# Sorted experts: who issues the loads of a block's rows and the stores of its results

## The chip, the cores and the metric

The kernel runs on one core of one Trainium2 chip. The metric is the device time in microseconds (us) of one execution. The kernel before was timed three times: 2738.66, 2728.6 and 2728.08 us, with a median of 2728.6 us.

The engines are named as the profile names them. PE is the matrix engine (PEld its weight load), DVE the vector engine, ACT the scalar engine, POOL is GpSimd, and SP is the synchronising engine, which in this kernel only issues transfers. An engine runs its own list of instructions strictly in order, and a wait on a semaphore holds back everything that stands behind it in that list.

## What is computed

The program is two dense transformer layers (`first_block`, in a loop over `DEPTH`) and then one block whose last part is a mixture of experts. 512 tokens of width 1024 are each sent to 2 of 16 experts:

```
gates = sum(one_hot(e_glob, 16) * weights)            # 2 of 16 per token
a = einsum('td,edf->tef', ht, w_e_gate)               # 1024 -> 256
u = einsum('td,edf->tef', ht, w_e_up)                 # 1024 -> 256
hid = silu(a) * u * gates[:, :, None]
out = hid.reshape(t, 16 * 256) @ w_e_down.reshape(16 * 256, d)
```

Everything is in float32. A product is made of three matrix products: each operand is split into a high part and a rest (`hi`, `lo`), and hi\*hi, lo\*hi and hi\*lo are added up.

## The kernel before

The change lies in `experts`, the last but one stage. The router has given each of the 1024 pairs of token and expert a row number (`slot`). GpSimd scatters the token rows into a table in HBM, `moe_in`, with eight indirect transfers (L2204). The table is sorted by expert and cut into 23 blocks of 128 rows: one block for each of the 16 experts, and 7 spill blocks for experts with more than 128 rows (`BLOCKS = EXPERTS + SPILLS`). For each block b the kernel loads 128 rows of 4 KB (0.52 MB) into `xb[b % 2]`, multiplies them with the weights of the expert, and stores 128 result rows (0.52 MB) from `y[b % 2]` into `moe_out` (L2214). After the last block `combine` gathers the results by eight indirect transfers (L2446). The weights of an expert are three transfers of 1.05 MB: two halves of gate and up (`load_gu`, L1979) and the down matrix (`load_down`, L1983). Weights, rows, results, split operands and sums all have two buffers.

The work of one block, by line:

- PE transposes the rows, `x_turn(b)`, eight operations (L2376); it waits for the load of the rows (`x_in`).
- ACT and DVE split the transposed rows (L2245, L2310) and the weights (L2253 and L2318 for the two halves of gate and up, L2268 and L2331 for down).
- PE makes gate and up, `up(b, 0)` and `up(b, 1)`, 12 matmuls each (L2389). ACT applies silu (L2275), DVE multiplies (`gated`, L2339).
- PE transposes the hidden rows, `h_turn(b)` (L2400), which ACT and DVE split (L2261, L2325).
- PE makes the output, `down(b)`, 12 matmuls (L2412), and ACT and DVE copy one half each into `y` (`y_half`, L2283 and L2347).

The engines are staggered by hand. In its iteration b each runs, in this order:

```
PE   x_turn(b+1)  up(b,0)  h_turn(b-1)  up(b,1)  down(b-1)
ACT  y_half(b-2)  x_hi(b+1)  w_hi(b+1,0)  h_hi(b-1)  w_hi(b+1,1)  down_hi(b)  gate(b)
DVE  y_half(b-2)  x_lo(b+1)  w_lo(b+1,0)  h_lo(b-1)  w_lo(b+1,1)  down_lo(b)  gated(b)
```

SP issues all the plain transfers of the stage. In its iteration b it waits until the rows of block b-2 are transposed and loads the rows of block b, waits for the split of the weights of b-2 and loads the weights of block b, and stores the results of block b-4 (`store_y`). So one list holds three kinds of transfer, and a store stands four blocks behind the load ahead of it. GpSimd does nothing between its eight scatters and the eight gathers of `combine`.

Of the kernel before, what the change touches and what calls it, by code (L numbers as in the profile page):

```python
# [26 lines left out]
P = 128  # L27
SEQ = 512
TB = SEQ // P
# [38 lines left out]
CHOSEN = 2  # L68
SPILLS = (CHOSEN * SEQ - EXPERTS) // P
BLOCKS = EXPERTS + SPILLS  # L70
# [2080 lines left out]
def experts(core, w_moe, rows, slot, spill_of):  # L2151
# [8 lines left out]
    with ExitStack() as st:  # L2160
# [10 lines left out]
        y = [rows[:, s, :] for s in range(2)]  # L2171
        xb = [rows[:, 2 + s, :] for s in range(2)]
# [4 lines left out]
        scattered = core.sem("moe_scattered", st)  # L2177
        x_in = [core.sem(f"moe_x_in{s}", st) for s in range(2)]
        x_turned = core.sem("moe_x_turned", st)
# [3 lines left out]
        gu_lo_done = core.sem("moe_gu_lo_done", st)  # L2183
        d_hi_done = core.sem("moe_d_hi_done", st)
        d_lo_done = core.sem("moe_d_lo_done", st)
# [7 lines left out]
        y_act = core.sem("moe_y_act", st)  # L2193
        y_dve = core.sem("moe_y_dve", st)
        y_out = [core.sem(f"moe_y_out{s}", st) for s in range(2)]
# [3 lines left out]
        with nc.Block() as block:  # L2199
            @block.gpsimd  # L2200
            def _(pool):
                for t in range(TB):
                    for n in range(CHOSEN):
                        nc.gpsimd.indirect_dma_start(  # L2204
                            out=core.moe_in[:, :], out_offset=bass.IndirectOffsetOnAxis(ap=slot[:, n, t:t + 1], axis=0),
                            in_=rows[:, t, :], in_offset=None).then_inc(scattered, 16)

            @block.sync
            def _(sp):
                def store_y(b):  # L2210
                    s = b % 2
                    sp.wait_ge(y_act, b + 1)
                    sp.wait_ge(y_dve, b + 1)
                    sp.dma_start(core.moe_out[b * P:(b + 1) * P, :], y[s]).then_inc(y_out[s], 16)  # L2214

                spills = [sp.value_load(spill_of[0:1, j:j + 1], min_val=0, max_val=EXPERTS - 1) for j in range(SPILLS)]
                sp.wait_ge(scattered, 16 * CHOSEN * TB)
                for b in range(BLOCKS):
                    s = b % 2
                    e = b if b < EXPERTS else spills[b - EXPERTS]  # L2220
                    if b >= 2:
                        sp.wait_ge(x_turned, b - 1)
                    sp.dma_start(xb[s], core.moe_in[b * P:(b + 1) * P, :]).then_inc(x_in[s], 16)
                    if b >= 2:
                        for h in range(2):
                            sp.wait_ge(gu_lo_done, 2 * (b - 2) + h + 1)
                            w_moe.load_gu(sp, e, s, h)
                        sp.wait_ge(d_lo_done, b - 1)
                        w_moe.load_down(sp, e, s)
                    if b >= 4:  # L2230
                        store_y(b - 4)
                for b in range(BLOCKS - 4, BLOCKS):
                    store_y(b)
                for s in range(2):
                    sp.wait_ge(y_out[s], 16 * len(range(s, BLOCKS, 2)))

            @block.scalar
            def _(act):
# [229 lines left out]
def second_block(core, w, out):  # L2468
    nc = core.nc
    x = core.x  # L2470
    with ExitStack() as blk:
# [84 lines left out]
        with ExitStack() as b:  # L2556
            rows = core.sb("moe_rows", [P, TB, D], ctx=b)
            share = core.sb("moe_share", [P, CHOSEN, TB], ctx=b)
            slot = core.sb("moe_slot", [P, CHOSEN, TB], mybir.dt.int32, ctx=b)
            spill_of = core.sb("moe_spill_of", [1, SPILLS], mybir.dt.int32, ctx=b)  # L2560
            w_moe = ExpertWeights(core, w, b)
            with ExitStack() as r:
                hi = core.sb("e_hi", [P, KD, SEQ], F32R, ctx=r)
                lo = core.sb("e_lo", [P, KD, SEQ], F32R, ctx=r)
                gain_row = core.sb("moe_gain_row", [P, D], ctx=r)
                transpose_split(core, "m2", x, hi, lo, KD, norm=True, ahead=w_moe.ahead,
                                rows=(rows, gain_row, w["ffn_gain2"].partition_broadcast(P)))
                route(core, w, hi, lo, share, slot, spill_of)
            experts(core, w_moe, rows, slot, spill_of)
            combine(core, share, slot, out)  # L2570
# [143 lines left out]
```

## Time and profile before

| what | value |
|---|---|
| median of three runs | 2728.6 us |
| the profiled execution, its time | 2734.79 us |
| the profiled execution, its span | 2733.0 us |
| granted clock of TensorE, mean of the span | 0.863 |
| PE, DVE, ACT, POOL busy | 83%, 51%, 32%, 13% |
| transfers of the span | 254.65 MB, 93 GB/s |

The profile is one execution; its time is 6.2 us above the median of the runs. A busy share over the whole span says little here, since the program is a row of stages with different limits. The stage of the experts is the stretch from about 2438 us to 2699 us of the span. In the views a line of a timeline begins with the start in us and the duration in us, then the engine, the line of the kernel, the operation, what it writes and reads, and how many instructions are merged in it; the bracket gives the idle time before it and what ended it. An engine name with a small q (SPq) is the issue of transfers.

### The profile page before, as it was taken

To read this page: it belongs to the slowest core of one execution; us is meant where nothing else is said; L and a number is where in the kernel's file an instruction comes from. 1 tells how busy PE (TensorE), PEld (TensorE's weight loads), DVE (VectorE), ACT (ScalarE), POOL (GpSimd) and SP (SyncE) were. 2 spreads that over 40 slices of the span, in tenths; PEclk is the share of its full clock that TensorE was granted. 3 is DMA by queue.
4 is the path that set the end of the run, shared out by engine and by line. 5 is a ranking of instruction groups with operands and counts; after the bars stand their busy time and mean duration, and the time that the engine had idled before them with its cause. 6 is when DMAs were issued, how large, how long until landed. Compare 5 with 4: busy or idle time off the path is not lost. (4 is left out here: it accounts for less than half of the span.)

```text
span 2733.0 us, 30197 instructions
## 1 busy us (share of the span) xinstructions
PE 2268.0 (83%) x11058; PEld 1826.6 (67%) x11058; DVE 1401.6 (51%) x2631; ACT 865.5 (32%) x1450; POOL 346.5 (13%) x263
## 2 busy tenths in 40 slices
PE   6888997999996888998899997997943766848884
PEld 6787775888886787776788886786631125737763
DVE  3675444444433566344444434224358964348875
ACT  3433333222212433332322212223214012136762
POOL 3553210000002544210000000000000000010001
PEclk9999786999997999687999998998555878869997
DMA  3101002322202111001322201220040002339995
GB/s 121 62 32 47 16 1 78 138 93 92 92 16 82 47 47 35 28 1 46 124 102 111 109 15 63 93 92 12 20 185 9 0 16 93 132 139 390 370 364 214
DMA packets 45308, 254.65 MB, mean 93 GB/s; under 512 B 6528, under 2 KB 6784, under 8 KB 21760
## 3 DMA queue, kind: packets, MB, share of 16 engines
q1 hardware_dynamic: 42880, 244.64, 24.3%
q0 software_dynamic: 2304, 8.39, 0.9%
q8 instruction: 74, 1.21, 0.2%
q14 instruction: 50, 0.41, 0.0%
HBM read 222.60 MB, written 30.41 MB: 93 GB/s over the span
## 5 line engine op out<-in xcount | busy, mean ns | idle before, releaser
L574 PE MATMUL ffn_up<-f_hi,ffn_gu_hi 128*128 128x512 f32 x704 | 275.9, 392 | 15.0 <-DVE ffn_gu_lo L545 12.2
L574 PE MATMUL ffn_up<-f_lo,ffn_gu_hi 128*128 128x512 f32 x704 | 275.3, 391 | 0.0
L574 PE MATMUL ffn_up<-f_hi,ffn_gu_lo 128*128 128x512 f32 x704 | 275.0, 391 | 0.0
L1365 PE MATMUL fill_ps<-mix_whi,h_hi 128*128 128x256 f32 (+1 forms) x704 | 213.2, 303 | 14.5 <-POOL mix_wlo L965 10.8
L1365 PE MATMUL fill_ps<-mix_whi,h_lo 128*128 128x256 f32 (+1 forms) x704 | 204.7, 291 | 0.0
L1365 PE MATMUL fill_ps<-mix_wlo,h_hi 128*128 128x256 f32 (+1 forms) x704 | 204.2, 290 | 0.0
L528 DVE TENSOR_TENSOR ffn_silu<-ffn_silu,ffn_up 128x512 f32<-128x512 f32 x44 | 30.2, 687 | 292.3 <-ACT ffn_silu L500 292.3
L1446 PE MATMUL o_ps<-values,prob_t 128*128 128x64 f32 x800 | 138.0, 315 | 50.6 <-DVE prob_t L1240 48.3
L1446 PEld LDWEIGHTS o_ps<-values,prob_t 128*128 128x128 f32 x800 | 131.4, 235 | 68.3 <-DVE prob_t L1240 58.4
L965 POOL TENSOR_TENSOR mix_wlo<-mix_raw,mix_whi 128x1024 fp32r<-128x1024 f32 x60 | 151.9, 2547 | 174.4 <-ACT mix_whi L1023 174.4
L574 PEld LDWEIGHTS ffn_up<-f_hi,ffn_gu_hi 128*128 128x128 f32 x704 | 133.1, 189 | 44.0 <-DVE ffn_gu_lo L545 12.7
L540 DVE TENSOR_TENSOR x<-ffn_down,x 128x512 f32<-128x512 f32 x176 | 119.7, 690 | 80.5 <-PE ffn_down L589 79.7
L1365 PEld LDWEIGHTS fill_ps<-mix_whi,h_hi 128*128 128x128 f32 x704 | 141.4, 201 | 26.8 <-POOL mix_wlo L965 11.6
L1231 DVE CUSTOM_DVE_ANT_0 s_ps<-s_ps,const 128x128 f32<-128x128 f32 (+1 forms) x124 | 58.9, 475 | 181.8 <-issue 181.8
L574 PEld LDWEIGHTS ffn_up<-f_hi,ffn_gu_lo 128*128 128x128 f32 x704 | 133.0, 189 | 27.8
L574 PEld LDWEIGHTS ffn_up<-f_lo,ffn_gu_hi 128*128 128x128 f32 x704 | 133.0, 189 | 27.6
L1365 PEld LDWEIGHTS fill_ps<-mix_whi,h_lo 128*128 128x128 f32 x704 | 141.6, 201 | 0.5
L1365 PEld LDWEIGHTS fill_ps<-mix_wlo,h_hi 128*128 128x128 f32 x704 | 141.1, 200 | 0.0
L1090 ACT ACTIVATE prob<-s_ps,neg_max 128x128 f32<-128x128 f32 (+3 forms) x160 | 84.5, 528 | 178.1 <-DVE neg_max L1231 178.0
L589 PE MATMUL ffn_down<-ffn_d_hi,ffn_hid_hi 128*128 128x512 f32 x352 | 136.9, 389 | 0.0
L589 PE MATMUL ffn_down<-ffn_d_hi,ffn_hid_lo 128*128 128x512 f32 x352 | 136.9, 389 | 0.0
L589 PE MATMUL ffn_down<-ffn_d_lo,ffn_hid_hi 128*128 128x512 f32 x352 | 136.9, 389 | 0.0
(428 smaller groups left out, 5187.9 us busy)
## 6 DMA issues: line engine op xcount, KB each, us to landing
moe_raw_gu<-in_w_e_gu SPq DMA_DIRECT2D x46, 1024.0 KB, 12.4
mix_raw<-in_w_mix SPq DMA_DIRECT2D x30, 1024.0 KB, 4.9
moe_raw_d<-in_w_e_down SPq DMA_DIRECT2D x23, 1024.0 KB, 8.7
ffn_raw_gu<-in_w_gate SPq DMA_DIRECT2D x22, 1024.0 KB, 4.9
ffn_raw_gu<-in_w_up SPq DMA_DIRECT2D x22, 1024.0 KB, 6.1
ffn_raw_d<-in_w_down SPq DMA_DIRECT2D x22, 1024.0 KB, 4.8
moe_in<-moe_empty SPq DMA_DIRECT2D x23, 512.0 KB, 8.3
moe_rows<-moe_in SPq DMA_DIRECT2D x23, 512.0 KB, 9.7
```

The lines of the kernel that those rows point to most:

```text
L528: nc.vector.tensor_tensor(act_t[:, b, :], act_t[:, b, :], up_ps[1][b][:], ALU.mult).then_inc(prod_done, 1)
L540: nc.vector.tensor_tensor(x_nt, down_ps[n % 4][:], x_nt, ALU.add).then_inc(added, 1)
L574: last = nc.tensor.matmul(up_ps[m][b][:], ww[:, m, k, b * P:(b + 1) * P], aw[:, k, :], start=n == 0, stop=n == 3 * KD - 1)
L589: last = nc.tensor.matmul(down_ps[n % 4][:], aw[:, k, t * P:(t + 1) * P], ww[:, k, c * 512:(c + 1) * 512], start=i == 0, stop=i == 3 * HB - 1)
L965: nc.gpsimd.tensor_tensor(w_lo[s][:, cols], w_raw[s][:, cols], w_hi[s][:, cols].bitcast(F32), ALU.subtract).then_inc(lo_done, 1)
L1090: nc.scalar.activation(prob[i][:], s_ps[n % 3][:, 0:(i + 1) * P], ACT.Exp, bias=neg_max[:, i:i + 1], scale=-1.0, accum_out=row_sum[a % 2][ ...
L1231: nc.vector.tensor_tensor_reduce(out=s, in0=s, in1=bias, scale=-(DIFF_D if DIF0 <= a < DSA0 else HEAD) ** -0.5, scalar=-NEG * 10, op0=ALU. ...
L1365: last = nc.tensor.matmul(b[:, 0:cols], aw[:, k, t * P:(t + 1) * P], ww[:, k, 0:cols], start=k == 0 and n == 0, stop=k == KD - 1 and n == 2)
L1446: last = nc.tensor.matmul(o_ps[:, i * HEAD:(i + 1) * HEAD], prob_t[n % 2][:, b * P:(b + 1) * P], val[:, b, v, :], start=b == 0, stop=b == i)
```

## The change

GpSimd's list goes on after the scatters: it waits for them itself, and then, for each block, loads the rows in and stores the results out. The store of block b-2 stands in the same iteration as, and behind, the load of block b. SP keeps the weights of blocks 2 to 22 alone; it waits no longer for the scatters, for the transposed rows or for the results. PE, ACT and DVE are not touched, nor are the buffers.

```diff
@@ -2204,35 +2204,31 @@
                             in_=rows[:, t, :], in_offset=None).then_inc(scattered, 16)
+                pool.wait_ge(scattered, 16 * CHOSEN * TB)
+                for b in range(BLOCKS + 2):
+                    s = b % 2
+                    if b < BLOCKS:
+                        if b >= 2:
+                            pool.wait_ge(x_turned, b - 1)
+                        pool.dma_start(xb[s], core.moe_in[b * P:(b + 1) * P, :]).then_inc(x_in[s], 16)
+                    if b >= 2:
+                        pool.wait_ge(y_act, b - 1)
+                        pool.wait_ge(y_dve, b - 1)
+                        pool.dma_start(core.moe_out[(b - 2) * P:(b - 1) * P, :], y[s]).then_inc(y_out[s], 16)
+                for s in range(2):
+                    pool.wait_ge(y_out[s], 16 * len(range(s, BLOCKS, 2)))
 
             @block.sync
             def _(sp):
-                def store_y(b):
-                    s = b % 2
-                    sp.wait_ge(y_act, b + 1)
-                    sp.wait_ge(y_dve, b + 1)
-                    sp.dma_start(core.moe_out[b * P:(b + 1) * P, :], y[s]).then_inc(y_out[s], 16)
-
                 spills = [sp.value_load(spill_of[0:1, j:j + 1], min_val=0, max_val=EXPERTS - 1) for j in range(SPILLS)]
-                sp.wait_ge(scattered, 16 * CHOSEN * TB)
-                for b in range(BLOCKS):
+                for b in range(2, BLOCKS):
                     s = b % 2
                     e = b if b < EXPERTS else spills[b - EXPERTS]
-                    if b >= 2:
-                        sp.wait_ge(x_turned, b - 1)
-                    sp.dma_start(xb[s], core.moe_in[b * P:(b + 1) * P, :]).then_inc(x_in[s], 16)
-                    if b >= 2:
-                        for h in range(2):
-                            sp.wait_ge(gu_lo_done, 2 * (b - 2) + h + 1)
-                            w_moe.load_gu(sp, e, s, h)
-                        sp.wait_ge(d_lo_done, b - 1)
-                        w_moe.load_down(sp, e, s)
-                    if b >= 4:
-                        store_y(b - 4)
-                for b in range(BLOCKS - 4, BLOCKS):
-                    store_y(b)
-                for s in range(2):
-                    sp.wait_ge(y_out[s], 16 * len(range(s, BLOCKS, 2)))
+                    for h in range(2):
+                        sp.wait_ge(gu_lo_done, 2 * (b - 2) + h + 1)
+                        w_moe.load_gu(sp, e, s, h)
+                    sp.wait_ge(d_lo_done, b - 1)
+                    w_moe.load_down(sp, e, s)
```

## Rows read from the trace of the kernel before

**Rows 1.** Windows; stretch, length, busy of PE, PEld, DVE, ACT, POOL, granted clock, DMA share, GB/s.

```profile
2462.90:2688.65 225.75, 199.33 (x922) 155.51 (x920) 185.05 (x162) 155.34 (x159) 0.00 (x0) 0.98 0.97 364
```

**Rows 2.** Waits of the stage, 2480 to 2720: who waited for what, us, times, longest.

```profile
PEld moe_xt_ps L2376 <- DMA moe_rows<-moe_in: 29.6, 18, 2.8
...
PE moe_xt_ps L2376 <- DMA moe_rows<-moe_in: 22.7, 14, 2.3
ACT moe_rows L2283 <- DMA moe_out<-moe_rows: 19.9, 14, 2.4
```

**Rows 3.** Timeline of DVE and PE: block 3 turned, the copies of y(0) and y(1).

```profile
2461.18 1.03 PE L2376 MATMUL moe_xt_ps<-const,moe_rows 128*128 128x128 f32 x8
...
2462.90 0.68 DVE L2347 COPY moe_rows<-moe_down_ps 128x512 f32<-128x512 f32 x1
...
2472.44 0.68 DVE L2347 COPY moe_rows<-moe_down_ps 128x512 f32<-128x512 f32 x1
```

**Rows 4.** Timeline of DVE: the copy of y(20), 20 copies after that of y(0).

```profile
2688.65 0.68 DVE L2347 COPY moe_rows<-moe_down_ps 128x512 f32<-128x512 f32 x1
```

**Rows 5.** Timeline of SP, the transfers around the copy of y(1).

```profile
2472.22 0.33 SPq L1983 DMA_DIRECT2D moe_raw_d<-in_w_e_down  x1
2472.66 0.37 SPq L2214 DMA_DIRECT2D moe_out<-moe_rows  x1
2473.07 0.43 SPq L2223 DMA_DIRECT2D moe_rows<-moe_in  x1
2473.54 1.76 SPq L1979 DMA_DIRECT2D moe_raw_gu<-in_w_e_gu  x2
```

**Rows 6.** Timeline of POOL and DVE: the first gathers of combine, in quiet transfers.

```profile
2704.03 0.97 POOL L2446 DMA_INDIRECT moe_got<-moe_out,moe_slot  x1 [272.35 <-PEq L2441]
2705.32 0.95 POOL L2446 DMA_INDIRECT moe_got<-moe_out,moe_slot  x1 [0.30 <-issue]
...
2708.47 1.28 DVE L2457 SCALAR_TENSOR_TENSOR x<-moe_got,moe_share,x 128x1024 f32<-128x1024 f32 x1 [8.87 <-DMA moe_got<-moe_out,moe_slot]
```

**Rows 7.** Timeline of POOL: the longest issue of a scatter.

```profile
2420.46 2.75 POOL L2204 DMA_INDIRECT moe_in<-moe_rows,moe_slot  x1 [0.30 <-issue]
```

**Rows 8.** Timeline of ACT and DVE: the steps from x_turn(3) to the copy of y(1).

```profile
2462.25 1.08 ACT L2245 CAST moe_xt_hi<-moe_xt_ps 128x512 fp32r<-128x512 f32 x2 [1.67 <-PE moe_xt_ps L2376]
2463.21 1.93 ACT L2253 CAST moe_gu_hi<-moe_raw_gu 128x2048 fp32r<-128x2048 f32 x1
2465.21 0.37 ACT L2261 CAST moe_ht_hi<-moe_ht_ps 128x256 fp32r<-128x256 f32 x1
2465.48 1.92 ACT L2253 CAST moe_gu_hi<-moe_raw_gu 128x2048 fp32r<-128x2048 f32 x1
...
2467.71 2.28 DVE L2318 TENSOR_TENSOR moe_gu_lo<-moe_raw_gu,moe_gu_hi 128x2048 fp32r<-128x2048 f32 x1
2469.91 2.29 DVE L2331 TENSOR_TENSOR moe_d_lo<-moe_raw_d,moe_d_hi 128x2048 fp32r<-128x2048 f32 x1
2472.11 0.41 DVE L2339 TENSOR_TENSOR moe_hid<-moe_silu,moe_up_ps 128x256 f32<-128x256 f32 x1
```

**Rows 9.** Windows, columns as in group 1: idle PE, and PE after it.

```profile
2310.00:2318.00 8.00, 0.00 (x0) 0.00 (x0) 7.32 (x13) 4.83 (x8) 0.00 (x0) 0.78 0.00 1
2318.00:2323.00 5.00, 0.00 (x0) 0.00 (x0) 3.62 (x6) 2.12 (x3) 0.00 (x0) 0.50 0.00 0
2323.00:2328.00 5.00, 4.77 (x22) 4.77 (x23) 3.58 (x4) 1.76 (x2) 0.00 (x0) 0.50 0.54 174
2328.00:2332.00 4.00, 4.00 (x35) 4.00 (x34) 0.85 (x2) 0.00 (x0) 0.00 (x0) 0.97 0.75 307
```

**Rows 10.** Timeline of PE: x_turn(1) at the low clock, and spacing of L2389 at both.

```profile
2442.61 1.94 PE L2376 MATMUL moe_xt_ps<-const,moe_rows 128*128 128x128 f32 x8 [2.09 <-DVE moe_xt_lo L2310]
...
2446.05 0.63 PE L2389 MATMUL moe_up_ps<-moe_gu_hi,moe_xt_lo 128*128 128x512 f32 x1
2446.48 0.63 PE L2389 MATMUL moe_up_ps<-moe_gu_lo,moe_xt_hi 128*128 128x512 f32 x1
...
2447.96 0.40 PE L2389 MATMUL moe_up_ps<-moe_gu_hi,moe_xt_hi 128*128 128x512 f32 x1
2448.19 0.40 PE L2389 MATMUL moe_up_ps<-moe_gu_hi,moe_xt_lo 128*128 128x512 f32 x1
```

**Rows 11.** Transfers issued in 2380 to 2733: count, KB each, median us to landing.

```profile
moe_raw_gu<-in_w_e_gu SPq DMA_DIRECT2D x42, 1024.0 KB, 12.5
moe_raw_d<-in_w_e_down SPq DMA_DIRECT2D x21, 1024.0 KB, 8.5
moe_rows<-moe_in SPq DMA_DIRECT2D x23, 512.0 KB, 9.7
moe_out<-moe_rows SPq DMA_DIRECT2D x23, 512.0 KB, 9.3
```

## The prediction

> **What bounds the kernel now.** I read the windows first, because the busy shares of the whole span mix stages. Between the copy of y(0) and the copy of y(20) the stage does 20 equal steps in 225.75 us, 11.29 us each [rows 1, 3, 4]. There the transfer engines are busy 97% of the time at 364 GB/s, and no compute engine comes near that: PE 199.33 us (88%), DVE 185.05 (82%), ACT 155.34 (69%) [rows 1]. A step moves three weight transfers of 1.05 MB and two of 0.52 MB, 4.19 MB. So the transfers bound the steady stretch. Below them lies a second floor: the two earliest copies of y, before the transfer queue has filled, stand 9.54 us apart [rows 3], which is what ACT's and DVE's chain takes when nothing comes late.
>
> The waits say the same. PE waits for a block's rows 14 times, 22.7 us, at most 2.3 us at once, and ACT 19.9 us for a store to free its buffer [rows 2]. These two waits are what the change is aimed at, and they are symptoms of a full queue: no byte is taken away.
>
> Third I read the order of one step. x_turn(3) starts at 2461.18 and the copy of y(0) at 2462.90 [rows 3]: PE turns block b+1 before DVE has copied y(b-2). This order is what the change touches.
>
> **The change, part by part.**
>
> *SP's list without rows and results.* SP's issue of a load or a store takes 0.37 to 0.43 us [rows 5], and SP mostly waits. In its new list a load of down weights still waits for d_lo(b), and both halves of the next gate and up stand right behind it with their own condition long true, since DVE makes gu_lo(b+1) before d_lo(b). So the weights go out when they go out now, a fraction of a us earlier. Worth nothing in the sum; if that cover were gone it would be 0.8 us a step.
>
> *The wait for the scatters.* SP no longer stands behind it, so gate and up weights of block 2 may leave earlier. Nothing waits for them that early. Zero.
>
> *The order on GpSimd's list.* This is the step that counts. GpSimd's iteration b is: load x(b), wait for y(b-2), store y(b-2). The next load, x(b+1), is queued behind the wait for y(b-2). And y(b-2) is copied from down(b-2), which is the last thing PE does in its iteration b-1; the first thing PE does in iteration b is x_turn(b+1). In SP's list the store was four blocks behind, y(b-4), and this wait was long over. In the new list PE ends down(b-2), then waits until DVE has copied y(b-2), GpSimd has issued the store and the load, and 0.52 MB have landed; up(b,0), h_turn and everything on ACT and DVE from x_hi(b+1) on stand behind x_turn(b+1) or its result. Two buffers of x help nothing, as the load is not allowed to go. Blocks 3 to 22 are hit: 20 steps, from y(0) to y(20).
>
> A new step is then a closed chain of two pieces.
>
> First piece, from x_turn to the next copy of y. x_turn(3) starts at 2461.18 and y(1)'s copy at 2472.44: 11.26 us, through x_hi, gu_hi, ht_hi, gu_hi on ACT and gu_lo, d_lo, hid on DVE [rows 3, 8]. That is with PE at the high clock. But PE's own work in it ends well before: its idle time per step would be about 10 us. In this trace PE idle from 2310 on has the clock at 0.50 of 2.4 GHz from 2318 on, and when work resumes at 2323 the clock stays at 0.50 for 5 us and is 0.97 in the next window [rows 9]. So I expect the first 5 us after each landing at 1.2 GHz. Eight transposes take 1.94 instead of 1.03, a matmul every 0.43 instead of every 0.23 [rows 3, 10]. In the 3.06 us left after x_turn run 7 matmuls of up(b,0), the other 5 take 1.15: 6.2; h_turn 0.4: 6.6; ht_hi 0.37: 7.0; the second gu_hi 1.92: 8.9; then DVE's starts 2.20, 2.20 and 0.33 apart [rows 3, 8]: the copy of y starts at 13.7 us. With the clock kept it is 11.26; these are the two ends, and I take 13.7, because an idle PE that long is what rows 9 show.
>
> Second piece, from the start of the copy of y to the next x_turn. No row of before has a plain transfer on GpSimd's queue. The nearest is the first gather of `combine`: the same queue, the same 128 rows of 4 KB, from HBM: issue at 2704.03, next issue 1.29 us later, used at 2708.47, so 4.44 us [rows 6]. Lower end: copy 0.68, store issued 1.29, load 4.44: 6.4 us. These gathers ran in quiet transfers. The new load does not: SP issues the down weights 0.22 us before the copy of y starts and both halves of gate and up within about 1.5 us after [rows 3, 5], 3.15 MB in front of and beside it. The store and the load are 1.05 MB together. With half of 430 GB/s (the 4.19 MB of a step in the 9.54 us of the fastest step would be 440) they take 4.9 us. Of the 4.44, 0.97 is issue, 1.22 transfer, 2.25 the way there and back; so data start at 0.68 + 0.97 + 1.1 = 2.7, end at 7.6 and are seen at 8.7 us. With a third of the rate, 7.3 us instead of 4.9: 11.1 us, the upper end (the 9.7 us that row loads take now in the full queue [rows 11], counted from an issue at 1.97, would give 11.7, but with 4.19 MB per step and over 20 us the queue no longer stays full). Half a share is the value nearest to two queues taking turns, and I take 8.7.
>
> The DMA page of the Trainium skill, "DMA: Bandwidth & Descriptors" (Queues, rings and completion order), says that an engine alternates between the queues that have work by whole packets, and that transfers from GpSimd and from SP lie in different queues. No row of before has both at full load. With turns by pieces of unlike length (a partition's 8 KB of weights against its 4 KB of rows, by the shapes of the loads) that rule leads to the upper end, which is a rival below.
>
> Sum: 13.7 + 8.7 = 22.4 us a step against 11.29, +11.1, times 20: +222 us. x(0) and x(1) leave GpSimd in 1.29 us instead of SP's 0.4, and the last stores too: +2. Total +224. On the profiled execution 2734.79 + 224 = 2959 us, on the median of the runs 2728.6 + 224 = 2953 us. What was gained on the way, the 22.7 and 19.9 us of waits, is inside the 11.29 and goes with it: the transfers are then idle half of the time.
>
> **The rivals.**
>
> *Quick landing.* The rows pass beside the weights and land at 6.4 us, PE still cold: 20.1 us a step, +176 +2: 2907 us. For it: the weights need only 7.3 us of a long step. Against: they are issued at exactly the same moment. 17%.
>
> *Clock kept.* 11.26 + 8.7 = 20.0 us a step, +173 +2: 2904 us; with quick landing as well 17.7 us, 2858 us. Against: rows 9. 10%.
>
> *Late landing.* A third of the rate: 13.7 + 11.1 = 24.8, +270 +2: 3001 us. 16%.
>
> *Slow issue.* If each issue on GpSimd took the 2.75 us of its slowest scatter [rows 7] instead of 0.97, 3.6 us more a step: +72 on the forecast, 3025 us. The Trainium skill, "SBUF — State Buffer" (Who interferes with whom), has GpSimd's descriptor writing shut out by certain DVE copies. Against: DVE stands still when GpSimd issues. 6%.
>
> *Faster.* The mechanism is the split of the queues: rows are no longer behind weights, PE's and ACT's waits of [rows 2] go, and the step falls to the 9.54 us of the chain: 20 x 1.75 = 35 us less, 2694 us. It decides from the point where x(b+1) has landed when PE ends down(b-2), that is, if the second piece were zero or less. The list forbids that, since the load is issued after a copy that comes after down(b-2). 4%. That both effects cancel or that the new list keeps the old time by some slack I overlooked: 2%, about 2729 us.
>
> **How the numbers follow.** The forecast, half share and cold PE, has 45%: 2953 us. Quick 17, clock kept 10, late 16, slow issue 6, faster 4, no change 2. The range from 2855 to 3015 takes in the first four cases besides the forecast and leaves out 12%; the ends of the unknown costs make it that wide. 0.5% is about what a measurement of this kernel tells from no change; faster by more 4%, within 2%, slower by more 94%.
>
> **What would show it.** In the profile after: PE waiting for moe_rows<-moe_in about 20 times for some 10 us each, the largest wait of the stage; copies of y 22 us apart; transfers at about half their rate in that stretch; the granted clock falling in the gaps, x_turn taking 1.94 us; row loads on the software queue (about 33 MB there instead of 8.39). If the copies stand 18 to 20 us apart, a size was wrong; if PE waits only 2 us for rows, the step on the order of GpSimd's list is wrong.

## The result and the profile after

The changed kernel takes 3032.6 us (median of four runs) against 2732.7 us for the kernel before in the same set of runs: a ratio of 1.110, with a 95% interval of 1.1065 to 1.1127. It is 300 us slower. The forecast was 2953 us and the range ended at 3015 us. The direction and the place were right; the size was not. Ratios, here and below, compare executions in the faster of two states that the chip shows; one execution in all fell in the other, one of the twelve of the kernel with the loads alone and the rows first (3174.6 us at a granted clock of 0.667), and its ratio leaves it out.

The profiled execution of the changed kernel took 3036.24 us, with a span of 3034.4 us. Its windows over the 20 steps from the copy of y(0) to the copy of y(20), with the columns of [rows 1]:

```profile
2472.51:2984.38 511.87, 232.72 (x928) 189.52 (x929) 187.10 (x161) 152.52 (x160) 21.30 (x40) 0.70 0.43 160
```

This answers [rows 1]. The same 20 steps take 511.87 us instead of 225.75. DVE and ACT are as busy as before, within 3 us. PE's busy time grew by 33 us; its first instructions in each step now run at the low clock, x_turn alone in 1.97 us instead of 1.03. The transfer engines are busy 43% of the time instead of 97%, and no compute engine is busy for half of it: no engine bounds the stretch now. The waits of the changed kernel between 2480 and 3010 us (who waited for what, us in total, times, longest) answer [rows 2]:

```profile
POOL moe_out L2217 <- DVE moe_rows L2343: 500.6, 22, 25.6
ACT moe_xt_hi L2241 <- PE moe_xt_ps L2372: 334.6, 20, 17.3
...
PE moe_xt_ps L2372 <- DMA moe_rows<-moe_in: 280.7, 20, 14.6
```

PE waits for rows 20 times, 14.0 us each on average, instead of at most 2.3 us. GpSimd stands nearly all of each step in front of the store, waiting for the copy of y, with the next load queued behind. One step of the timeline (start, duration, engine, line, operation), over SP, GpSimd, DVE, ACT and the first PE work:

```profile
2601.80 0.68 DVE L2343 COPY moe_rows<-moe_down_ps 128x512 f32<-128x512 f32 x1
2601.95 0.92 SPq L1979 DMA_DIRECT2D moe_raw_gu<-in_w_e_gu  x2
2603.04 0.54 POOL L2217 DMA_DIRECT2D moe_out<-moe_rows  x1 [24.97 <-DVE moe_rows L2343]
2603.56 0.54 POOL L2213 DMA_DIRECT2D moe_rows<-moe_in  x1
2614.42 1.97 PE L2372 MATMUL moe_xt_ps<-const,moe_rows 128*128 128x128 f32 x8 [14.12 <-DMA moe_rows<-moe_in]
...
2619.88 0.37 ACT L2257 CAST moe_ht_hi<-moe_ht_ps 128x256 fp32r<-128x256 f32 x1 [0.56 <-PE moe_ht_ps L2396]
...
2626.84 0.68 DVE L2343 COPY moe_rows<-moe_down_ps 128x512 f32<-128x512 f32 x1
```

From the copy of y to x_turn it is 12.6 us, and 12.4 from there to the next copy. This is one of the shorter steps: over all 20 the two pieces take 12.5 and 13.1 us on average, the second between 12.4 and 13.9. Where [rows 3] had x_turn of block 3 ahead of the copy of y(0), x_turn now comes after the copy each time. The windows of that gap, with the columns of [rows 9]:

```profile
2602.00:2604.00 2.00, 0.00 (x0) 0.00 (x0) 0.49 (x1) 0.00 (x0) 0.96 (x2) 0.92 0.67 176
2604.00:2606.00 2.00, 0.00 (x0) 0.00 (x0) 0.00 (x0) 0.00 (x0) 0.10 (x1) 0.50 1.00 401
...
2612.00:2614.00 2.00, 0.00 (x0) 0.00 (x0) 0.00 (x0) 0.00 (x0) 0.00 (x0) 0.50 0.85 352
2614.00:2616.00 2.00, 1.58 (x8) 1.58 (x9) 0.00 (x0) 0.00 (x0) 0.00 (x0) 0.50 0.00 0
2616.00:2618.00 2.00, 2.00 (x8) 1.69 (x7) 0.95 (x2) 1.57 (x3) 0.00 (x0) 0.66 0.00 0
2618.00:2620.00 2.00, 2.00 (x12) 1.63 (x11) 0.98 (x2) 1.44 (x2) 0.00 (x0) 1.00 0.00 0
```

Between 2604 and 2614 the five transfers of the step run at 326 to 426 GB/s and no engine computes. After 2614 nothing moves. The rows are the last to land, 10.8 us after their issue and so at 2614.4; the weights of gate and up, issued from 2601.95 on, take 9.7 us in this step. The clock is 0.50 in the gap and 1.00 from 2618 on. The transfers issued between 2500 and 2960 (count, KB each, median us to landing):

```profile
moe_raw_gu<-in_w_e_gu SPq DMA_DIRECT2D x35, 1024.0 KB, 10.9
moe_raw_d<-in_w_e_down SPq DMA_DIRECT2D x17, 1024.0 KB, 5.0
moe_out<-moe_rows POOLq DMA_DIRECT2D x18, 512.0 KB, 9.0
moe_rows<-moe_in POOLq DMA_DIRECT2D x18, 512.0 KB, 10.9
```

The last of the 20 steps is a control inside the changed kernel: SP has only the down weights of the last block left to issue (2963.50), and from the copy of y at 2963.58 to x_turn it is 7.6 us, the whole step 20.8.

The 301.4 us between the two profiled spans divide as follows: 286.1 in the 20 steps (511.87 less 225.75); 4.9 between the first scatter and the copy of y(0) (48.9 against 44.0); 5.7 between the copy of y(20) and the end (50.0 against 44.35); and 4.7 ahead of the first scatter, where nothing was changed. In the profiles of all the kernels here the first scatter starts anywhere between 2410 and 2424 us, so these 4.7 us say nothing of the change.

### The profile page after: what moved, and what is told of

It reads as the page before. It is cut to its first block and busy times, and to the rows that moved or that the text cites. A ratio compares the mean times of both kernels' runs of the same rounds, so it can differ in the third digit from the quotient of the medians.

```text
span 3034.4 us, 30197 instructions
## 1 busy us (share of the span) xinstructions
PE 2301.4 (76%) x11058; PEld 1859.3 (61%) x11058; DVE 1403.8 (46%) x2631; ACT 862.3 (28%) x1450; POOL 371.7 (12%) x309
## 5 line engine op out<-in xcount | busy, mean ns | idle before, releaser
L2372 PE MATMUL moe_xt_ps<-const,moe_rows 128*128 128x128 f32 x184 | 44.3, 421 | 312.6 <-DMA moe_rows<-moe_in 310.5
L2372 PEld LDWEIGHTS moe_xt_ps<-const,moe_rows 128*128 128x128 f32 x184 | 35.5, 220 | 321.6 <-DMA moe_rows<-moe_in 319.0
L1365 PE MATMUL fill_ps<-mix_whi,h_hi 128*128 128x256 f32 (+1 forms) x704 | 214.7, 305 | 14.5 <-POOL mix_wlo L965 10.8
L2306 DVE TENSOR_TENSOR moe_xt_lo<-moe_xt_ps,moe_xt_hi 128x512 fp32r<-128x512 f32 x46 | 29.7, 687 | 313.2 <-ACT moe_xt_hi L2241 313.2
L574 PEld LDWEIGHTS ffn_up<-f_hi,ffn_gu_hi 128*128 128x128 f32 x704 | 133.1, 189 | 44.0 <-DVE ffn_gu_lo L545 12.7
L1365 PEld LDWEIGHTS fill_ps<-mix_whi,h_hi 128*128 128x128 f32 x704 | 142.8, 203 | 28.0 <-POOL mix_wlo L965 11.6
## 6 DMA issues: line engine op xcount, KB each, us to landing
moe_in<-moe_empty SPq DMA_DIRECT2D x23, 512.0 KB, 11.1
moe_rows<-moe_in POOLq DMA_DIRECT2D x23, 512.0 KB, 10.9
```

Source lines behind the costliest of these rows:

```text
L574: last = nc.tensor.matmul(up_ps[m][b][:], ww[:, m, k, b * P:(b + 1) * P], aw[:, k, :], start=n == 0, stop=n == 3 * KD - 1)
L1365: last = nc.tensor.matmul(b[:, 0:cols], aw[:, k, t * P:(t + 1) * P], ww[:, k, 0:cols], start=k == 0 and n == 0, stop=k == KD - 1 and n == 2)
L2306: nc.vector.tensor_tensor(xt_lo[s][:, h * HK:(h + 1) * HK, :], xt_ps[h][:].rearrange("p (k n) -> p k n", k=HK), xt_hi[s][:, h * HK:(h + 1) ...
L2372: last = nc.tensor.transpose(xt_ps[k // HK][:, (k % HK) * P:(k % HK + 1) * P], xb[s][:, k * P:(k + 1) * P], ident)
```

## The experiments

My theory was the order on GpSimd's list: the load of x(b+1) stands behind the wait for y(b-2). The rival was the queue: rows on GpSimd's queue are served last beside the weights, in whatever order they are issued. The ratios below are to the kernel before, timed again in the same set of runs (17 or 19 executions, medians of 2734.6 to 2734.8 us).

**Store of b-4 on GpSimd.** The order alone is put back; the engines stay as changed.

```diff
-                for b in range(BLOCKS + 2):
+                for b in range(BLOCKS + 4):
...
-                    if b >= 2:
-                        pool.wait_ge(y_act, b - 1)
-                        pool.wait_ge(y_dve, b - 1)
-                        pool.dma_start(core.moe_out[(b - 2) * P:(b - 1) * P, :], y[s]).then_inc(y_out[s], 16)
+                    if b >= 4:
+                        o = b - 4
+                        pool.wait_ge(y_act, o + 1)
+                        pool.wait_ge(y_dve, o + 1)
+                        pool.dma_start(core.moe_out[o * P:(o + 1) * P, :], y[o % 2]).then_inc(y_out[o % 2], 16)
```

> GpSimd keeps all loads of rows and stores of results, but the store in its iteration b is that of block b-4, as it was on SP, instead of b-2. Order theory (the load of x(b+1) is queued behind the copy of y(b-2), which comes after down(b-2)): the coupling is gone, a step falls from 25.6 us to at most the 11.3 us of before, 2700 to 2745 us in all. Queue theory (rows are slow because GpSimd's queue is served last beside the weights, whatever the order): row loads still land 10 us and more after issue and PE keeps waiting, 2850 us or more.

Measured: 2729.4 us, ratio to the kernel before 0.9969 (0.9951 to 0.9987). All of the 300 us are gone, and the waits between 2480 and 2680 us have no line of PE for rows. The windows from the copy of y(0) to that of y(20) in this kernel, columns as above:

```profile
2470.82:2680.98 210.16, 193.92 (x918) 154.61 (x917) 184.57 (x161) 153.84 (x159) 20.26 (x38) 0.99 0.98 386
```

10.5 us a step, with GpSimd's queue carrying rows and results. In its transfers (count, KB, median us to landing) a row load takes longer to land than in the changed kernel, 12.4 us against 10.9:

```profile
moe_out<-moe_rows POOLq DMA_DIRECT2D x15, 512.0 KB, 9.5
moe_rows<-moe_in POOLq DMA_DIRECT2D x15, 512.0 KB, 12.4
```

A late landing costs nothing where the load is issued early enough. The queue theory falls as the cause of the 300 us.

The 20 steps take 15.6 us less than before (210.16 against 225.75), but the whole gains only 5 us by the medians, 0.3% by the ratio. The start and the end stay as in the changed kernel: 49.0 us from the first scatter to the copy of y(0) and 49.6 from the copy of y(20) to the end, each 5 us more than before.

**Store of b-3.** As above, with 3 in place of 4.

```diff
-                for b in range(BLOCKS + 2):
+                for b in range(BLOCKS + 3):
...
-                    if b >= 2:
+                    if b >= 3:
+                        o = b - 3
```

> As the kernel with the store of b-4, but the store in iteration b is that of b-3. Order theory: the load of x(b+1) now hangs on the copy of y(b-3), one step earlier, so two steps must hold one landing (12.6 us from the copy to the next x_turn in the profile after) and one pass from x_turn to a copy (11.3 us): 12.0 us a step, about 0.7 more than before, 2740 to 2765 us. If only the queue mattered it would be like the store of b-2, 3030 us.

Measured: 2782.9 us, ratio 1.0171 (1.0142 to 1.02). The effect is there, but larger than expected: 13.2 us a step instead of 12.0. The steps come in pairs, one short and one long (9.8 and 17.2 us in these rows of its timeline):

```profile
2653.18 0.68 DVE L2343 COPY moe_rows<-moe_down_ps 128x512 f32<-128x512 f32 x1
...
2654.94 0.54 POOL L2212 DMA_DIRECT2D moe_rows<-moe_in  x1
...
2663.00 0.69 DVE L2343 COPY moe_rows<-moe_down_ps 128x512 f32<-128x512 f32 x1
...
2667.26 1.97 PE L2372 MATMUL moe_xt_ps<-const,moe_rows 128*128 128x128 f32 x8 [5.80 <-DMA moe_rows<-moe_in]
...
2680.19 0.68 DVE L2343 COPY moe_rows<-moe_down_ps 128x512 f32<-128x512 f32 x1
```

The chain holds two steps for one landing, as expected. The expectation had 12.6 us from the copy to x_turn and 11.3 from there. In these rows it is 14.1 (2653.18 to 2667.26) and 12.9; over the ten pairs it is 13.1 and 13.3 on average. So most of the miss is the clock: PE went cold in the wait, 1.97 us for x_turn. The landing adds 0.5 us a pair.

**Loads alone on GpSimd, stores with SP.** One part of the change alone.

```diff
-                    if b >= 2:
-                        pool.wait_ge(y_act, b - 1)
-                        pool.wait_ge(y_dve, b - 1)
-                        pool.dma_start(core.moe_out[(b - 2) * P:(b - 1) * P, :], y[s]).then_inc(y_out[s], 16)
...
                     w_moe.load_down(sp, e, s)
+                    if b >= 4:
+                        store_y(b - 4)
```

> GpSimd issues the loads of rows alone; SP keeps the weights and, four blocks behind, the stores. Order theory: no load waits for a result, so as fast as before or a little faster, 2700 to 2740 us. Queue theory: rows on GpSimd's queue land late, PE waits, 2850 us or more.

Measured: 2734.4 us, ratio 0.9997 (0.9979 to 1.0015): no difference. The half of the change that moves the loads is harmless; the harm comes with the stores of b-2 that stand between them.

**PE kept busy in the gap.** 52 matmuls into an unused bank (`idle_ps`) stand ahead of each wait for rows.

```diff
+FILL = 52
...
                     s = b % 2
+                    if b >= 3:
+                        for n in range(FILL):
+                            nc.tensor.matmul(idle_ps[:], xt_hi[s][:, n % KD, :], gu_hi[s][:, n % KD, :], start=True, stop=True)
                     pe.wait_ge(x_in[s], 16 * (b // 2 + 1))
```

> The changed kernel with 52 matmuls of 512 columns into an unused bank ahead of each wait for rows from block 3 on (52 x 0.228 = 11.9 us at the high clock), so PE has work in most of the gap. Clock theory (part of the loss is PE at 1.2 GHz after each gap): x_turn takes 1.03 instead of 1.97 us and x_turn to the copy of y 11.3 instead of 12.4 to 13.7, so 20 to 45 us less than the changed kernel, 2990 to 3012 us. If the low clock is hidden behind the casts and subtractions: within 5 us of the changed kernel's 3032.

Measured: 3007.9 us, ratio 1.1002 (1.097 to 1.1033), 25 us less than the changed kernel. One step, and the windows in it:

```profile
2706.23 0.68 DVE L2345 COPY moe_rows<-moe_down_ps 128x512 f32<-128x512 f32 x1
...
2718.79 1.09 PE L2377 MATMUL moe_xt_ps<-const,moe_rows 128*128 128x128 f32 x8 [2.34 <-DMA moe_rows<-moe_in]
...
2730.11 0.69 DVE L2345 COPY moe_rows<-moe_down_ps 128x512 f32<-128x512 f32 x1
```

```profile
2715.00:2720.00 5.00, 2.66 (x17) 2.04 (x16) 0.00 (x0) 0.08 (x1) 0.00 (x0) 1.00 0.62 258
2720.00:2725.00 5.00, 5.00 (x24) 4.07 (x23) 3.46 (x3) 4.91 (x6) 0.00 (x0) 1.00 0.01 3
```

With the clock at 1.00 it is 11.3 us from x_turn to the copy, the value of [rows 3], and still 12.6 us from the copy to x_turn. That holds for 15 of the 20 steps. In the other five the clock fell around x_turn all the same (0.66 of full speed from 2792 to 2797, for one), and it is 12.5 to 12.7 us. So 25 us of the changed kernel's loss came back with the clock kept in three steps of four; kept in all of them it would be some 35 us, an estimate from 13.1 less 11.3 in 20 steps. The rest is the chain.

**No weight loads after the first two blocks.** SP's loop is left out and the waits for weights are for the first ones, so blocks 2 to 22 compute with the weights of experts 0 and 1.

```diff
-                for b in range(2, BLOCKS):
...
-                    w_moe.load_down(sp, e, s)
+                sp.wait_ge(gu_lo_done, 1)
...
-                    act.wait_ge(gu_in[s][h], 16 * (b // 2 + 1))
+                    act.wait_ge(gu_in[s][h], 16)
...
-                    act.wait_ge(d_in[s], 16 * (b // 2 + 1))
+                    act.wait_ge(d_in[s], 16)
```

> The changed kernel without the weight loads of blocks 2 to 22: those blocks compute with the weights of experts 0 and 1, which stay in their buffers, so 66 MB of transfers are left out. GpSimd's list is as in the changed kernel. If rows land late because 3.15 MB of weights go at the same moment: from the copy of y to x_turn falls from 12.6 to about 6 us (copy 0.68, wake-up 0.56, store issued 0.54, load landed 4.0 to 4.5), a step from 25.6 to 18.5 to 19.5, in all 2890 to 2915 us. If the landing is slow by GpSimd's queue itself: over 3000 us. Either way clearly above the kernel before, as the order alone makes the chain.

Measured: 2913.3 us, ratio 1.0647 (1.0625 to 1.0669). One step:

```profile
2659.74 0.68 DVE L2335 COPY moe_rows<-moe_down_ps 128x512 f32<-128x512 f32 x1
2660.97 0.54 POOL L2217 DMA_DIRECT2D moe_out<-moe_rows  x1 [19.22 <-DVE moe_rows L2335]
2661.50 0.54 POOL L2213 DMA_DIRECT2D moe_rows<-moe_in  x1
2666.24 1.97 PE L2364 MATMUL moe_xt_ps<-const,moe_rows 128*128 128x128 f32 x8 [8.03 <-DMA moe_rows<-moe_in]
```

6.5 us from the copy to x_turn, which is the lower end of the prediction (6.4), and 13.9 from there to the next copy at 2680.12 (13.7 in the prediction). On average over the 20 steps it is 6.6 and 13.4, a step of 20.0 us. So about 6 us of each step of the changed kernel are the weights' company (25.6 less 20.0), and almost 9 are the chain itself (20.0 less 11.3).

**Queues swapped.** SP issues rows and results in the changed order, GpSimd the weights (with semaphores of their own from block 2 on).

```diff
-                        pool.dma_start(xb[s], core.moe_in[b * P:(b + 1) * P, :]).then_inc(x_in[s], 16)
+                        sp.dma_start(xb[s], core.moe_in[b * P:(b + 1) * P, :]).then_inc(x_in[s], 16)
...
-                        pool.dma_start(core.moe_out[(b - 2) * P:(b - 1) * P, :], y[s]).then_inc(y_out[s], 16)
+                        sp.dma_start(core.moe_out[(b - 2) * P:(b - 1) * P, :], y[s]).then_inc(y_out[s], 16)
...
-                        w_moe.load_gu(sp, e, s, h)
+                        w_moe.load_gu(pool, e, s, h)
```

> Queues swapped, order kept: SP issues rows and results in the changed kernel's order (store of b-2 ahead of the load of b+1), GpSimd, after its scatters, the weights. Order theory: still one closed chain per block, 2900 us or more. On the size: if rows land late because GpSimd's queue gets the smaller share, the rows on SP's queue now land in 5 to 7 us after issue and a step is 19 to 21 us, 2900 to 2940 us; if rows get the smaller share because their pieces are 4 KB against 8 KB, whatever the queue, the step stays near 25 us, 3010 to 3040 us.

Measured: 3018.3 us, ratio 1.1029 (1.1007 to 1.1051). Rows on SP's queue land 11.6 us after issue, weights on GpSimd's 5.9 and 10.7, nearly as with the queues the other way round. Its transfers (count, KB, median us to landing):

```profile
moe_raw_gu<-in_w_e_gu POOLq DMA_DIRECT2D x32, 1024.0 KB, 10.7
moe_raw_d<-in_w_e_down POOLq DMA_DIRECT2D x16, 1024.0 KB, 5.9
moe_out<-moe_rows SPq DMA_DIRECT2D x16, 512.0 KB, 8.2
moe_rows<-moe_in SPq DMA_DIRECT2D x16, 512.0 KB, 11.6
```

So the chain does not need its transfers on GpSimd's list. The medians alone would say that neither queue is the favoured one and that rows end last because their pieces are shorter. The steps of this run say more. In this one GpSimd issues the down weights with the copy of y and the next ones 0.55 us ahead of the rows:

```profile
2722.92 0.54 POOL L1983 DMA_DIRECT2D moe_raw_d<-in_w_e_down  x1 [24.67 <-DVE moe_d_lo L2330]
2723.45 1.07 POOL L1979 DMA_DIRECT2D moe_raw_gu<-in_w_e_gu  x2
2724.00 0.43 SPq L2228 DMA_DIRECT2D moe_rows<-moe_in  x1
2736.11 1.97 PE L2375 MATMUL moe_xt_ps<-const,moe_rows 128*128 128x128 f32 x8 [14.72 <-DMA moe_rows<-moe_in]
```

From the down weights of block 16 on, the first spill block, they come some 0.4 us later against the copy of y, here at 2825.47:

```profile
2825.87 0.54 POOL L1983 DMA_DIRECT2D moe_raw_d<-in_w_e_down  x1 [22.50 <-DVE moe_d_lo L2330]
2826.46 1.13 POOL L1979 DMA_DIRECT2D moe_raw_gu<-in_w_e_gu  x2
2826.59 0.43 SPq L2228 DMA_DIRECT2D moe_rows<-moe_in  x1
2836.73 1.97 PE L2375 MATMUL moe_xt_ps<-const,moe_rows 128*128 128x128 f32 x8 [12.75 <-DMA moe_rows<-moe_in]
```

In the six full steps of this kind the copy is 11.1 to 11.4 us ahead of x_turn, in the thirteen before them 12.7 to 13.2, and the transfers go on for another 1.3 us after the rows are in. With the same pieces and the same queues, 0.4 us in the order of issue moved the landing by almost 2 us. So the moment of issue counts, and the length of the pieces is not shown to.

**Queues swapped, store of b-4.** The same with the order of the kernel before.

```diff
-                for b in range(BLOCKS + 2):
+                for b in range(BLOCKS + 4):
...
-                    if b >= 2:
+                    if b >= 4:
+                        o = b - 4
```

> Queues swapped as in the kernel before this one, but with the store of b-4. Order theory: no chain, 2710 to 2750 us. If weights on GpSimd's queue come late beside rows on SP's, ACT waits for weights and it is 2760 us or more.

Measured: 2727.8 us, ratio 0.9975 (0.9957 to 0.9993). The order decides here too.

**Rows first.** All transfers are made, but the weights wait until the rows have landed.

```diff
                     sp.wait_ge(d_lo_done, b - 1)
+                    sp.wait_ge(x_in[s], 16 * (b // 2 + 1))
                     w_moe.load_down(sp, e, s)
```

> The changed kernel, and SP waits until the rows of block b have landed before it issues the down weights of b and the gate and up weights of b+1. All transfers are made, only their order in time differs. If rows land late because the weights are issued at the same moment: from the copy of y to x_turn is 6.5 us as without weight loads (the 2913 us run), a step about 20 us, 2905 to 2925 us; the weights still land in the remaining 13 us. If weights then come late for ACT, or the slow landing came from something else: 2950 us or more.

Measured: 2921.6 us, ratio 1.0675 (1.0659 to 1.0691). One added wait takes 111 us off the changed kernel. From the copy at 2650.10 to x_turn it is 6.5 us again, and a step is 20.0 us:

```profile
2650.10 0.68 DVE L2344 COPY moe_rows<-moe_down_ps 128x512 f32<-128x512 f32 x1
2651.86 0.54 POOL L2213 DMA_DIRECT2D moe_rows<-moe_in  x1
2656.57 1.97 PE L2373 MATMUL moe_xt_ps<-const,moe_rows 128*128 128x128 f32 x8 [7.99 <-DMA moe_rows<-moe_in]
2656.61 0.33 SPq L1983 DMA_DIRECT2D moe_raw_d<-in_w_e_down  x1
```

The late landing is therefore the company of the weights issued at the same moment, in a kernel that computes everything.

**The start: SP's wait for the scatters.** Put back, on top of the store of b-4.

```diff
+                sp.wait_ge(scattered, 16 * CHOSEN * TB)
                 for b in range(2, BLOCKS):
```

> The kernel with GpSimd storing b-4, and SP's wait for the scatters put back ahead of the weights of block 2. If these weights, issued under the scatters since the change, delay the last scatter and so block 0 (in the profile after GpSimd waits 8.26 us for the scatters after its last issue, before SP 3.6 us), this saves about 5 us of the 2729 us: 2720 to 2727. If not: 2729 within 3 us, or a few us more because the weights of block 2 leave later.

Measured: 2728.3 us, ratio 0.9975 (0.9964 to 0.9986), the same as without the wait. The scatters do end sooner: the first row load goes out 4.8 us after the last scatter's issue instead of 9.2 (2433.93 less 2429.17; 2442.86 less 2433.65). But the weights of block 2 then leave at the same moment as x(0), which takes 8.6 us from issue to x_turn instead of 3.6 (2446.47 less 2442.86 without the wait):

```profile
2433.66 0.81 SPq L1979 DMA_DIRECT2D moe_raw_gu<-in_w_e_gu  x2
2433.93 1.15 POOL L2212 DMA_DIRECT2D moe_rows<-moe_in  x2 [3.81 <-DMA moe_in<-moe_rows,moe_slot]
2442.53 1.97 PE L2373 MATMUL moe_xt_ps<-const,moe_rows 128*128 128x128 f32 x8 [30.41 <-DMA moe_rows<-moe_in]
```

The 4.4 us saved are spent again. The kernel without weight loads has neither: there the copy of y(0) stands 44.6 us behind the first scatter, where it stands 48.9 in the changed kernel and 49.5 here.

**The start: rows of blocks 0 and 1 ahead of the weights of block 2.** Tried on the loads alone and on the swapped queues with the store of b-4, where the added wait stands in GpSimd's list.

```diff
+                for s in range(2):
+                    sp.wait_ge(x_in[s], 16)
                 for b in range(2, BLOCKS):
```

> GpSimd issues the loads of rows alone, SP weights and stores four blocks behind, and SP waits for the rows of blocks 0 and 1 before the weights of block 2. Start theory (weights of block 2 under the scatters cost 5 us; released at the end of the scatters they delay x(0) by the same 5 us): now neither happens and the copy of y(0) stands 44 us behind the first scatter instead of 49, so about 5 us less than loads alone, 2722 to 2730 us. If not: 2734 within 3 us.

Measured: 2732.3 us, ratio 0.9985 (0.9972 to 0.9998).

> Rows and results on SP with the store of b-4, weights on GpSimd, which waits for the rows of blocks 0 and 1 before the weights of block 2. Start theory: about 5 us less than the same kernel without that wait (2727.8), 2719 to 2726 us, the fastest of all. If not: 2728 within 3 us.

Measured: 2725.7 us, ratio 0.9963 (0.9948 to 0.9978). In both the copy of y(0) stands 44 to 45 us behind the first scatter (2454.01 less 2410.15 in the second), where it stood 49, so the start is as expected. The whole gains 2 us of the 5, which these runs can't tell from nothing; the first kernel is above its expected range (2722 to 2730), the second at the top of its own (2719 to 2726). Where the rest goes isn't shown: in the profiled executions the 20 steps behind the start take 9.7 us more in the first kernel (225.17 against 215.52 with the loads alone) and the same in the second (217.52 against 217.37). The last kernel has the lowest time of all, 0.4% below the kernel before; its interval overlaps those of the two other kernels with the store of b-4 and an unchanged start.

## Why the prediction was right in place and wrong in size

*What bounds the kernel now.* Right. The transfers set the steady stretch; with rows and results issued on their own list and in good order a step falls from 11.3 to 10.5 us at 386 GB/s, and the whole gains 0.3%, since two thirds of it are lost again at the start and at the end.

*The order on GpSimd's list.* Right: 20 steps, blocks 3 to 22, one closed chain each. Taking away the order alone takes away the whole loss.

*First piece, x_turn to the copy.* Forecast 13.7 us, measured 13.1 on average, since the clock came back 3 to 5 us after x_turn's start instead of always 5 (in the rows above, 0.66 in 2616 to 2618, 1.00 from 2618); the longest took 13.9. With the clock kept it was 11.3, as stated. 0.6 us too much a step, -12 us.

*Second piece, the copy to x_turn.* This is the step that failed. Forecast 8.7 us with half the rate for rows and results; measured 12.5 on average, 12.8 in the 19 steps that have all the weights beside them. The sum assumed that store and load get half of the rate and so end well before the weights. In fact all 4.19 MB of a step go through in about 11 us and the rows end with the last of them, while the down weights land after 5.0 us. The upper end, 11.1 us with a third of the rate, was nearer and still short. It left out 0.56 us from the end of the copy to GpSimd's store (2602.48 to 2603.04), but also had the issue 0.43 us too long, so the two nearly cancel. What is left is the share: with the way there and back of the prediction, the 1.05 MB of the step shown above had from 2.9 to 11.5 us behind the copy, 122 GB/s or 28% of 430. This is an estimate, and nearer to the quarter that they are of the step's bytes than to a third. The lower end came out, at 6.5 us where weights don't go at the same time, partly by luck: 0.56 us of wake-up was left out, issue was 1.07 for two transfers instead of 2.26, and the landing took longer. 3.8 us too little a step, +76 us.

The rule of the Trainium skill that was weighed there ("DMA: Bandwidth & Descriptors", Queues, rings and completion order: an engine alternates between queues by packets) would have given 3001 us. The trace agrees with it in that rows get less than half beside the weights on either queue, but they got less than a third too, and in the swapped run the landing moved by almost 2 us with the moment of issue. By which rule the engines share is left open.

*The wait for the scatters.* Forecast zero, "nothing waits for them that early". Wrong: the two weight loads that SP could now send early run under the scatters, which land 4.7 us later (GpSimd waits 8.26 us for them; SP issued its first load 3.6 us after the last scatter before). With SP's wait put back GpSimd waits 3.81 us, and without weight loads the start is as short as before. Nobody waits for the weights, but somebody waited for what they push aside.

*The end.* Forecast within the +2; measured 5.7. With the last stores on GpSimd's queue the first gather comes 9.8 us after the last copy of y starts (3005.28 less 2995.51), with the stores on SP's 5.1 [rows 6] (2704.03 less 2698.91). It goes with the stores in every kernel here: 9.8 us in the seven that have them on GpSimd's queue, 4.5 to 5.1 in the six that have them on SP's, also where GpSimd issues the weights. The last store lands 2.9 us after its issue either way, and from 3001 to 3005 nothing moves. What GpSimd does in that time isn't shown.

Together: 76 - 12 us in the steps, 4.9 at the start, 5.7 less the forecast 2 at the end, and 4.7 ahead of the stage that belong to no change, 77 us: the 301 measured against the 224 forecast. The rivals: quick landing was the state of two experiments and not of the change; clock kept gave back 25 us in a run that kept it in three steps of four, and would be worth some 35 and not 49; slow issue, whose 3025 us lies nearest to the measured time, never appeared: GpSimd's plain issue took 0.54 us in every step, half of what the gathers had suggested.

The range was too narrow by the same step: it put 3001 us as the far case and left out that the small terms at the start and at the end both lie on the slow side.

## What to carry to other kernels

Before moving transfers to another engine's list, write out which wait stands in front of each load and which instruction ends it; a prefetch that is queued behind a store is no prefetch, whatever buffers there are, and one place more of distance for the store took back 250 of the 300 us, two places all of them. When a transfer becomes part of a closed chain, price its late end as that of the last byte of everything issued at the same moment, and see what stands ahead of it: 0.4 us in the order of issue was worth almost 2. A load that is released earlier is not free because nobody waits for it: ask what it will run beside.

## What the runs showed of the hardware

A plain transfer of 128 rows of 4 KB on GpSimd's queue is issued in 0.54 us, the indirect one mostly in 0.95, and it lands within 0.2 us of one on SP's queue: x(0) is used 3.5 us after its issue here (2448.16 less 2444.63), 3.3 us on SP (2438.55 less 2435.25). GpSimd's store starts 0.56 us after the end of the copy that it waits for, SP's, in the swapped queues, 0.07 us (2723.63 after a copy from 2722.88 to 2723.56).

Rows issued up to 2 us behind 3.15 MB of weights landed 10.9 us after issue on GpSimd's queue and 11.5 to 12.1 on SP's, and in 4.7 us when only the results went beside them; on SP's queue, with the weights issued 0.4 us later, it was 9.9 to 10.2.

After a last store on GpSimd's queue its first gather came 9.8 us behind the start of the last copy of y, after one on SP's 4.5 to 5.1.
